# Single-transfer SSM scratch with re-ordered channels, and the output projection's copies issued from the POOL queue

## What is computed

```python
proj = jnp.einsum('bld,de->ble', xn, w_in)
q, k, v, u = jnp.split(proj, [D_ATTN, D_ATTN + D_KV, D_ATTN + 2 * D_KV], axis=-1)
attn = sliding_window_attention(q, k, v, sinks)              # window 128, 16 heads, rotary
y = s5_ssm(u.reshape(B, L, N_SSM_GROUPS, SSM_GROUP), ...)    # 64 groups of 16 channels
z = jax.nn.gelu(y)
ssm = z * jax.nn.sigmoid(jnp.einsum('blc,ce->ble', z, w_glu) + b_glu)
mixed = jnp.concatenate([rms_norm(attn, g_attn_out), rms_norm(ssm, g_ssm_out)], axis=-1)
h = x + rms_norm(mixed @ w_o, g_post_mix)
out = h + rms_norm(swiglu(rms_norm(h, g_pre_ffn), w_gate, w_up, w_down), g_post_ffn)
```

## Time and profile before

| | |
|---|---|
| median of 3 runs | 2618.92 us (2614.8 to 2630.63) |
| the profiled execution: its time, its span | 2622.94 us, 2621.4 us (core 2, the slowest; the 8 cores' spans are 2590.2 to 2621.4 us) |
| busy TensorE, DVE, ACT, POOL | 94%, 60%, 32%, 22% of the span |
| transfers | 341.82 MB; from POOL's queue 173.10 MB, from SP's 166.57 MB |
| the chain that ended last | TensorE 82%, transfers 7%, DVE 4% |

### The profile page before, as it was taken

One profiled execution on the slowest core, in us unless ns is written; L12 is line 12 of the kernel. 1 busy time (PEld: TensorE's weight loads), 2 busy tenths in 40 slices (PEclk: granted clock), 3 DMA queues, 4 the chain that ended last, 5 costly groups with the idle time before them and its releaser, 6 DMA issues.

```text
span 2621.4 us, 33797 instructions; the slowest of 8 cores (2590.2 to 2621.4 us)
## 1 busy us (share of the span) xinstructions
PE 2469.1 (94%) x12896; PEld 1209.5 (46%) x12896; DVE 1559.8 (60%) x2436; ACT 829.8 (32%) x1634; POOL 567.3 (22%) x650
## 2 busy tenths in 40 slices
PE   4999788978989889999999999999999999999998
PEld 2546557833434434444444444444444444444443
DVE  7866674758767778777777400017888887710003
ACT  5544443367555433222222100003322223200002
POOL 0244635744333201000010111100100101111112
PEclk9888779989999999999999999999999999999999
DMA  9687948465776977766667977749999976775566
GB/s 246 164 132 118 109 79 112 87 162 158 187 201 176 200 136 129 95 82 90 88 85 93 185 108 109 106 74 155 177 177 179 136 90 82 96 119 74 79 105 234
DMA packets 479773, 341.82 MB, mean 130 GB/s; under 512 B 182016, under 2 KB 442496, under 8 KB 470656
## 3 DMA queue, kind: packets, MB, share of 16 engines
q0 software_dynamic: 260944, 173.10, 49.0%
q1 hardware_dynamic: 218672, 166.57, 25.0%
HBM read 406.65 MB, written 63.96 MB: 180 GB/s over the span
## 4 chain that ended last, share of the span: by engine, by line
PE 82%; DMA 7%; DVE 4%; issue 2%; ACT 2%; POOL 1%; SPq 1%; POOLq 0%; DVEq 0%
PE ps L433 82%; DMA ws.6_48<-w_in 2%; SPq L433 1%; DMA PT.127_169<-Pb.124_166 1%; DVE ast.27_69 L433 1%; DMA PT.127_169<-Pb.123_165 1%; DVE ast.26_68 L433 1%; DMA raw.149_191<-w_up 1%; DMA zraw.109_151<-zscr 1%; DMA raw.147_189<-w_gate 1%; DVE xr.138_180 L433 0%; DMA xt.33_75<-x 0%; DVE xr.139_181 L433 0%; DVE attn.128_170 L433 0%; POOL hf.235_277 L433 0%
## 5 line engine op out<-in xcount | busy, mean ns | idle before, releaser
L433 ACT ACTIVATE ps<-ps 128x512 f32<-128x512 f32 x96 | 55.8, 581 | 347.8 <-DVE ev.176_218 L433 138.5
L433 DVE TENSOR_TENSOR hf.235_277<-ps,gpo.190_232 128x512 f32<-128x512 f32 x16 | 11.1, 692 | 244.8 <-ACT junk.145_187 L433 235.1
L433 PE MATMUL ps<-hnT.144_186,wsm.152_194 128*128 128x512 bf16 x528 | 121.1, 379 | 0.0
L433 PE MATMUL ps<-hnT.144_186,wsm.154_196 128*128 128x512 bf16 x528 | 121.1, 379 | 0.0
L433 PE MATMUL ps<-hnT.144_186,wsm.153_195 128*128 128x512 bf16 x528 | 121.1, 379 | 0.0
L433 PE MATMUL ps<-hnT.144_186,wsm.151_193 128*128 128x512 bf16 x528 | 121.0, 379 | 0.0
L433 DVE TENSOR_TENSOR wsm.154_196<-raw.150_192 128x1024 bf16<-128x1024 bf16 x110 | 69.0, 686 | 79.8 <-DMA raw.150_192<-w_gate 77.7
L433 ACT ACTIVATE junk.145_187<-ps 128x512 bf16<-128x512 f32 x16 | 9.6, 597 | 254.8 <-PE ps L433 254.8
L433 PEld LDWEIGHTS ps<-hnT.144_186,wsm.154_196 128*128 128x128 bf16 x528 | 51.7, 98 | 62.3
L433 PEld LDWEIGHTS ps<-hnT.144_186,wsm.153_195 128*128 128x128 bf16 x528 | 51.7, 98 | 62.3
L433 PEld LDWEIGHTS ps<-hnT.144_186,wsm.152_194 128*128 128x128 bf16 x528 | 51.7, 98 | 62.3
(11 more groups left out here) (1373 smaller groups left out, 6211.6 us busy)
## 6 DMA issues: line engine op xcount, KB each, us to landing
raw.147_189<-w_gate POOLq DMA_DIRECT2D x22, 1024.0 KB, 9.2
raw.148_190<-w_up POOLq DMA_DIRECT2D x22, 1024.0 KB, 9.3
raw.150_192<-w_gate POOLq DMA_DIRECT2D x22, 1024.0 KB, 12.2
raw.149_191<-w_up POOLq DMA_DIRECT2D x22, 1024.0 KB, 11.9
woscr<-w_o POOLq DMA_DIRECT2D x16, 512.0 KB, 9.5
xr.138_180<-x SPq DMA_DIRECT2D x8, 1024.0 KB, 6.2
xr.139_181<-x SPq DMA_DIRECT2D x8, 1024.0 KB, 6.5
hscr<-xr.138_180 SPq DMA_DIRECT2D x8, 1024.0 KB, 4.8
```

What stands on the lines that cost most here:

```text
L433: inst = getattr(eng, m)(*a, **kw)
```

## The change

Channels within a block of 128 are renumbered: row i of a block now holds channel 16 * (i % 8) + i // 8 of it. The host permutes the columns of `w_in`, both sides of `w_glu`, the lower rows of `w_o`, and two small vectors. With that order, partition (j, p) of a block is one contiguous run of 4096 bytes in `uscr` and `zscr`, so the eight loads and the eight stores of a block become one transfer each. `zst` gets a second tile. `oproj`'s load of x and store of h are issued from POOL's queue. Unit 2 of the feed-forward part loads its weights into a place of its own at 162 KB (the place of `Wo[6]`, the seventh piece of the output projection's weights). The arithmetic is the same.

```diff
-    uscr = dscr("uscr", [8, 1024, 256], BF16)
-    zscr = dscr("zscr", [8, 1024, 256], BF16)
+    uscr = dscr("uscr", [8, 8, 128, 256], BF16)
+    zscr = dscr("zscr", [8, 8, 128, 256], BF16)
@@ proj_u
-                    c0 = (4 * h + blk) * 128
-                    P.dma(uscr[:, c0:c0 + 128, :].rearrange("j p c -> p j c"), ust[:, 3 - blk, :, :], q="gpsimd", wk=[("u", 4 * h + blk)])
+                    P.dma(uscr[4 * h + blk].rearrange("j p c -> p j c"), ust[:, 3 - blk, :, :], q="gpsimd", wk=[("u", 4 * h + blk)])
-        zst = sb("zst", SO + 28 * KB, [128, 8, 256], BF16)
+        zst = [sb("zst", o_, [128, 8, 256], BF16) for o_ in (SO + 28 * KB, c1 + 2944)]
@@ ssm_pair
-                for j in range(8):
-                    P.dma(uring[b8 % 2][16 * j:16 * j + 16, :, :],
-                          uscr[j, b8 * 128:(b8 + 1) * 128, :].rearrange("(g p) c -> p g c", p=16), rk=[("u", b8)],
-                          wk=[("ur", b8, j)])
+                P.dma(uring[b8 % 2][:, :, :].rearrange("p g c -> p (g c)"),
+                      uscr[b8].rearrange("j (p g) c -> (j p) (g c)", g=8), rk=[("u", b8)], wk=[("ur", b8)])
-                for j in range(8):
-                    P.dma(zscr[j, b8 * 128:(b8 + 1) * 128, :].rearrange("(g p) c -> p g c", p=16),
-                          zst[16 * j:16 * j + 16, :, :], wk=[("z", b8, j)])
+                P.dma(zscr[b8].rearrange("j (p g) c -> (j p) (g c)", g=8), zs[:, :, :].rearrange("p g c -> p (g c)"),
+                      wk=[("z", b8)])
@@ oproj
-            P.dma(xr[:, :], x[tt * 128:(tt + 1) * 128, :])
+            P.dma(xr[:, :], x[tt * 128:(tt + 1) * 128, :], q="gpsimd")
-            P.dma(hscr[tsl, :], xr[:, :], wk=[("h", tt)])
+            P.dma(hscr[tsl, :], xr[:, :], q="gpsimd", wk=[("h", tt)])
@@ unit
+        raw2 = sb("raw", 162 * KB, [128, 16, 256], BF16)
+            if blk == 0 and u == 2:
+                r = raw2
@@ _host_layouts
+    r = np.arange(1024)
+    pm = (r // 128) * 128 + 16 * (r % 8) + (r % 128) // 8
+    w_in = np.concatenate([inp["w_in"][0][:, :1536], inp["w_in"][0][:, 1536:][:, pm]], axis=1)
+    w_glu = inp["w_glu"][0][pm][:, pm]
+    w_o = np.concatenate([inp["w_o"][0][:1024], inp["w_o"][0][1024:][pm]], axis=0)
```

More of the change, by code:

```diff
@@ L884, in ssm_pair @@
             if q % 4 == 0:
-                for j in range(8):
-                    P.dma(uring[b8 % 2][16 * j:16 * j + 16, :, :],
-                          uscr[j, b8 * 128:(b8 + 1) * 128, :].rearrange("(g p) c -> p g c", p=16), rk=[("u", b8)],
-                          wk=[("ur", b8, j)])
+                P.dma(uring[b8 % 2][:, :, :].rearrange("p g c -> p (g c)"),
+                      uscr[b8].rearrange("j (p g) c -> (j p) (g c)", g=8), rk=[("u", b8)], wk=[("ur", b8)])
+            zs = zst[b8 % 2]
             AT, CL, KT, U = A1Ts[b8 % 3], CLs[b8 % 3], KTs[b8 % 3], uring[b8 % 2]
@@ L927, in ssm_pair @@
                 g = 2 * q + par
-                V.scalar_tensor_tensor(out=zst[:, g8 + par, :], in0=U[:, g8 + par, :],
+                V.scalar_tensor_tensor(out=zs[:, g8 + par, :], in0=U[:, g8 + par, :],
                                        scalar=sm[:, C_DSK + g:C_DSK + g + 1], in1=ps[:, 6 + par, 0:256],
@@ L945, in zconv @@
                 zr = zraw[b % 2]
-                P.dma(zr[:, :, :], zscr[:, b * 128:(b + 1) * 128, :].rearrange("j p c -> p j c"),
-                      rk=[("z", b, j) for j in range(8)], wk=[("zr", b)])
+                P.dma(zr[:, :, :], zscr[b].rearrange("j p c -> p j c"), rk=[("z", b)], wk=[("zr", b)])
                 for h in range(2):
@@ L1312, in build_nc @@
         V.memset(v1[:, 1:17, :, 64:65], 1.0)
-        ur = [("ur", 1, j) for j in range(8)]
+        ur = [("ur", 1)]
         P.prio = 59.0
@@ L1385, in _host_layouts @@
     sm[:, C_SINK:C_SINK + 16] = inp["sinks"][0][None, :]
-    sm[:, C_GSSM:C_GSSM + 8] = inp["g_ssm_out"][0].reshape(8, 128).T
-    sm[:, C_BGLU:C_BGLU + 8] = inp["b_glu"][0].reshape(8, 128).T
     sm[:, C_KT:C_KT + 17] = np.concatenate([np.arange(7, -1, -1), np.arange(0, 9)]).astype(f32)[None, :]
@@ L1407, in _host_layouts @@
     gv[4, :1024] = inp["g_attn_out"][0]
+    r = np.arange(1024)
[3 more added lines that the diff above has]
+    w_o = np.concatenate([inp["w_o"][0][:1024], inp["w_o"][0][1024:][pm]], axis=0)
+    sm[:, C_GSSM:C_GSSM + 8] = inp["g_ssm_out"][0][pm].reshape(8, 128).T
+    sm[:, C_BGLU:C_BGLU + 8] = inp["b_glu"][0][pm].reshape(8, 128).T
     return {
@@ L1411, in _host_layouts @@
         "b2": b2.reshape(128, 2, 512), "c2": c2.reshape(128, 2, 512),
-        "w_in": np.ascontiguousarray(inp["w_in"][0]), "w_glu": np.ascontiguousarray(inp["w_glu"][0]),
-        "w_o": np.ascontiguousarray(inp["w_o"][0]), "w_gate": np.ascontiguousarray(inp["w_gate"][0]),
+        "w_in": np.ascontiguousarray(w_in), "w_glu": np.ascontiguousarray(w_glu),
+        "w_o": np.ascontiguousarray(w_o), "w_gate": np.ascontiguousarray(inp["w_gate"][0]),
         "w_up": np.ascontiguousarray(inp["w_up"][0]), "w_down": np.ascontiguousarray(inp["w_down"][0]),
```

## The result

The changed kernel takes **2688.95 us** in the median (2687.7 to 2692.7) against 2617.03 for the kernel before in the same comparison: a ratio of **1.026, 95% interval 1.021 to 1.031**, or +72 us. Predicted were 2583 us, range 2558 to 2608, with 8% for slower. The profile is that of core 0, now the slowest.

A forecast was written before the change was run, and what follows sets the result against it. The prediction took PE as the bound, full for 62% of the span, with idle time and lost clock in the SSM and output projection. SSM -23, output projection -5, unit 2's weights -7.5 took 2618.9 to 2583 us, range 2558 to 2608.

The forecast's parts named there:

- Output projection, -5 us: Output projection: copies off SP end the transposes' stalls, -8, less +3 for POOL's issues; between -13 and +10 us.
- set it aside at 4%: Rival, 4%: moving copies to POOL gives nothing, as transposes stall on full DMA engines from whichever queue; 2588 us.
- POOL's issues, +3: Output projection: 32 more issues on POOL, about 1.14 us each, make some masks late; +3 us, ends 0 and +36.5.
- two `PT` tiles and three `Pb` tiles stand between: Output projection: the reason given that few masks made late by POOL's new issues reach PE.
- The slower rival, 8%, 2651 us: Output projection, 8%: POOL is held up by its own waits, 14 loads at 4.5 us, 63 us; 2651 us.
- SSM, -23: SSM, 281 to 425 us: single transfers and a second `zst` tile cut PE's waits; -23 us, between -8 and -45.
- `uring` gave 1.8 of 7.9: SSM: the single load lands after 4.3 us, so PE's whole `uring` wait goes, -7.9 us.
- `zst` 4.2 of the 5 taken: SSM: the second tile removes DVE's 11.0 us wait; PE's 7.3 us `zst` wait shrinks by 5.
- `zraw` 0.1 of 6: SSM: the `zraw` load should no longer collide with q weight loads; -6 us of PE's 9.1 us wait, less sure.
- give nothing: Stages before the SSM stretch: PE has no wait on these transfers on core 2, so no change in time.
- DVE and the new list take the place: SSM rival, 28%: steps between PE and DVE bound the pairs, removed waits return as `Rb` and `pab` waits; 2602 us.
- Unit 2's weights, -7.5: Feed-forward unit 2: load goes 6.6 us earlier, PE waits 3.5 us instead of 10.1; -7.5 us, between -4 and -12.

The follow-up runs named there:

- the small load: Kernel before with the load of x on POOL's queue, but only 128 of 2048 columns of each tile loaded: 0.9996.
- a longer wait: Kernel before with the load of x on POOL's queue, waiting also until the `hn` transpose of the tile two before has landed: 1.0015.
- the SSM part: Kernel before with renumbered channels, one `uring` load and one `zscr` store a block, two `zst` tiles: profiled execution 2626.13 us, no ratio of its own.
- the third `A1`: A third 2 KB buffer A1, used in turn: 0.9938 added to the kernel before with the SSM part, 0.9952 added to the kernel before alone.

## Why the prediction was wrong, step by step

- **Output projection, -5 us, was +59.5 (mean of the cores). This step failed.** I read in the earlier trace rows that SP is held 5.34 us behind a load of x and concluded that the load's place in SP's queue was the cause; "With the copies gone from SP only transposes follow each other there, and these cost 1.23" is the sentence that is false: `hnT` held SP for 5.9 to 6.6 us at nine of eleven places (core 0, 640 to 886 us). The transposes are held by the bytes in flight, from whichever queue. The Trainium skill's "DMA: Bandwidth & Descriptors", section "Issuing engines are not separate DMA queues", which I cited, says that transfers of all issuing engines run on the same 16 DMA engines and interleave. These runs agree, and I had set it aside at 4% because a row seemed to speak against it; it did not, since the row only shows that a transpose behind a load is late, and a load from either queue does that (6.16 us from SP, 6.11 from POOL). With the rule alone, though, the part comes out at 0, not at +60. What it needed besides was the price of a late transpose in the new lists: 12 `PT` of 40 land late before and after, but PE's waits for them grew from 8.4 to 48.4 us. A sign stood in the section on the change: in POOL's new list the load stands right behind a pair of masks, beside the `PT` that they free and the `hnT` behind it.
- **POOL's issues, +3, and "two `PT` tiles and three `Pb` tiles stand between".** POOL's busy time rose by 9 us in the stretch (102.5 to 111.9, with fewer tiles done in it), an issue of x costs it 0.55 us and not 1.14. This term was harmless: the store alone on POOL is 1.0009, the small load 0.9996.
- **The slower rival, 8%, 2651 us.** Right in sign, wrong in mechanism: POOL's waits cost nothing (0.9996 with a small load, 1.0015 with a longer wait).
- **SSM, -23.** SP issues store and load within 0.8 to 1.6 us on the eight cores, as forecast. Of the waits, `uring` gave 1.8 of 7.9 (the landing takes 10.6 to 20.2 us, not 4.3), `zst` 4.2 of the 5 taken, `zraw` 0.1 of 6. Of the -23, 8 us were to come from the clock; no run shows them, 29.0 us are lost to it in that stage before and 29.6 in the SSM part. And I wrote that the stages ahead "give nothing": they lost 8.0 us, since the weight loads that wait for `uring` start earlier. The rival "DVE and the new list take the place" describes the sum, though what DVE waited for was a transfer. Nor does the gain appear once that wait is gone: with the third `A1` the kernel is 0.9938 with the single transfers and 0.9952 without.
- **Unit 2's weights, -7.5.** The load goes out 6 us earlier (core 0: 0.7 us behind the last store of `h` before, 5.2 us ahead of it with this edit alone), as forecast, and brings 3.8 us of wait: the term was twice too large, just outside my bound of -4.
- **The sum.** Summed were -35.5 us. The changed kernel with the copies on SP measured +3 (1.0010), and the copies on POOL added the rest of the +72.

## What to carry to other kernels

Before a large copy is moved to another queue, ask beside which small transfers it will leave then, and how soon each of them is needed: from the shared queue the copy made transposes late as well, but PE hardly waited for them. And when a transfer is made to land earlier, look for all that waits for it: here two weight loads did, and they landed on a transpose for which PE, behind DVE, stood 8 to 14 us. Where an engine waits to overwrite what a transpose reads, try one more small buffer: here it gave 0.5% where holding the transfers back gave nothing.

## What was unexpected of the hardware

- A DMA transpose issued beside a 1 MB copy lands about 1 us after the copy (copy 6.8, transpose 7.6 us; 2.7 to 4.5 at most other places), and the next transpose on SP, one of `hn`, holds SP for 5.9 to 6.6 us instead of 1.7. It happens whether the copy comes from POOL's queue or from SP's (6.16 us).
- With more in flight it is later still: transposes landed after 26.0, 26.5 and 25.2 us beside a copy and weight loads. A 512 KB load in pieces of 4096 bytes took 20.2 us on core 7 of the SSM part, and one like it, issued at 318.6 us, 4.1; with 512-byte pieces the median is 4.3. So the size of the pieces did not show; what else was in flight did.
